# First attention of a two-block model: the reciprocal one unit late, transposes and values one unit later, and each head's values on its own half of the array's columns by turns

## The reference, cut to what matters

```
rows = s // GRID_W                      # 16 rows of 64 tokens
row_start = np.clip(r - kh // 2, 0, rows - kh)
scores = jnp.einsum('bhrnqd,bhrnikd->bhrnqik', q_blk, kg).astype(jnp.float32)
scores = scores + bias[None]
scores = jnp.where(valid[:, :, None, :], scores, -1e30)
probs = jax.nn.softmax(scores, axis=(-2, -1)).astype(v.dtype)
out = jnp.einsum('bhrnqik,bhrnikd->bhrnqd', probs, vg)
```

## Time and profile before

| what | value |
|---|---|
| median of three executions | 4185.94 us |
| the profiled execution's own time | 4187.09 us |
| its span in the trace | 4185.3 us |
| TensorE busy over the span | 3963.6 us, 95% |
| VectorE, ScalarE, GpSimd busy | 43%, 25%, 17% |
| the attention of this change | about 192 to 387 us of the span |
| mean granted TensorE clock | 0.964 of full speed |

### The profile page before, as it was taken

One profiled execution on the slowest core, in us unless ns is written; L12 is line 12 of the kernel. 1 busy time (PEld: TensorE's weight loads), 2 busy tenths in 40 slices (PEclk: granted clock), 3 DMA queues, 4 the chain that ended last, 5 costly groups with the idle time before them and its releaser, 6 DMA issues. The chain is left out here.

```text
span 4185.3 us, 42926 instructions
## 1 busy us (share of the span) xinstructions
PE 3963.6 (95%) x16912; PEld 2751.7 (66%) x16912; DVE 1783.1 (43%) x3155; ACT 1049.6 (25%) x1797; POOL 692.6 (17%) x533
## 2 busy tenths in 40 slices
PE   8988999999999999999997998988999998999998
PEld 4465444444458888877555888745678747888886
DVE  2165776533032233224447898356642123322232
ACT  1043553000022211223332332114431112122210
POOL 1053000000001100111002011004420112333333
PEclk9999999999999999998998998899899999999999
DMA  3200102334011111122101212200002201111111
GB/s 144 58 1 3 38 10 71 101 111 141 30 41 42 50 51 51 51 72 76 53 6 29 41 31 54 96 16 1 1 23 72 85 18 60 51 51 48 44 51 51
DMA packets 200181, 211.42 MB, mean 51 GB/s; under 512 B 64560, under 2 KB 152240, under 8 KB 199600
## 3 DMA queue, kind: packets, MB, share of 16 engines
q1 hardware_dynamic: 140624, 172.50, 12.5%
q10 hardware_dynamic: 59360, 36.19, 3.2%
HBM read 185.33 MB, written 21.50 MB: 49 GB/s over the span
## 5 line engine op out<-in xcount | busy, mean ns | idle before, releaser
L95 PE MATMUL ps<-halves 128*128 128x512 f32 x7296 | 1665.0, 391 | 23.3 <-DVE halves L378 11.0
L95 PEld LDWEIGHTS ps<-halves 128*128 128x128 f32 x7296 | 1374.7, 189 | 312.2 <-issue 11.4
L95 PE MATMUL ps<-arena 128*128 128x512 f32 (+4 forms) x4208 | 1448.2, 501 | 65.2 <-DVE arena L544 25.0
L95 PEld LDWEIGHTS ps<-arena 128*128 128x128 f32 (+1 forms) x4208 | 721.9, 190 | 736.2 <-issue 667.4
L1265 DVE TENSOR_TENSOR halves<-tmps,halves 128x512 fp32r<-128x512 f32 x128 | 88.6, 692 | 525.2 <-ACT halves L1220 525.2
L1244 POOL TENSOR_TENSOR tmps<-tmps 128x512 f32<-128x512 f32 x128 | 137.7, 1076 | 1000.7 <-ACT tmps L1212 1000.7
L1151 ACT ACTIVATE halves<-raws 128x2048 fp32r<-128x2048 f32 x62 | 118.4, 1909 | 559.9 <-PE ps L95 524.6
L889 POOL TENSOR_TENSOR arena<-arena 128x512 f32<-128x512 f32 x32 | 41.9, 1311 | 939.7 <-DVE arena L860 691.2
L1251 POOL TENSOR_TENSOR arena<-arena 128x512 f32<-128x512 f32 x128 | 164.7, 1294 | 191.3 <-DVE arena L1288 191.3
L1158 DVE TENSOR_TENSOR halves<-raws,halves 128x2048 fp32r<-128x2048 f32 x62 | 142.2, 2293 | 73.6 <-ACT halves L1151 73.6
L1212 ACT ACTIVATE tmps<-ps 128x512 f32<-128x512 f32 x128 | 76.5, 598 | 377.6 <-PE ps L95 377.6
(11 more groups left out here) (272 smaller groups left out, 3549.8 us busy)
## 6 DMA issues: line engine op xcount, KB each, us to landing
arena<-in_w_in SPq DMA_DIRECT2D x16, 2048.0 KB, 9.0
raws<-in_w_ff SPq DMA_DIRECT2D x31, 1024.0 KB, 5.4
raws<-in_w_mlp SPq DMA_DIRECT2D x31, 1024.0 KB, 5.2
arena<-in_w_ada ACTq DMA_DIRECT2D x24, 1024.0 KB, 5.2
arena<-in_w_out SPq DMA_DIRECT2D x4, 2048.0 KB, 11.0
mixw<-in_w_in SPq DMA_DIRECT2D x16, 512.0 KB, 4.1
h_stash<-arena SPq DMA_DIRECT2D x1, 5120.0 KB, 20.8
inverses<-arena ACTq DMA_DIRECT2D x20, 256.0 KB, 2.9
```

Of the source, the lines that this page charges most:

```text
L95: ins = e.matmul(out_ap, l, r, start=i == 0, stop=i == n - 1)
```

## The change

Three things change, all in the four functions of the attention. First, VectorE computes the reciprocal of unit `i-1` in iteration `i`, behind bias and maximum of unit `i`. Second, transposes and evacuation are those of unit `i-3`, values and copies out those of unit `i-4`; `pbuf` gets a fifth buffer for that. Third, the values of a unit are no longer four matmuls with 128 by 128 weights but eight with 128 by 64: each head has its own 64 feature columns, 64 query rows moving, and its own half of the output partitions, the two heads by turns. Both results then lie in columns 0 to 63 of the bank, so that one copy of 128 by 64 takes the place of two of 64 by 64.

```diff
@@ tensor_natt
-            for i in range(64 + 3):
+            for i in range(64 + 4):
...
-                if 0 <= i - 2 < 64:
-                    u = i - 2
+                if 0 <= i - 3 < 64:
+                    u = i - 3
                     key = ("at", u)
...
-                if 0 <= i - 3 < 64:
-                    u = i - 3
+                if 0 <= i - 4 < 64:
+                    u = i - 4
                     r, j, start = natt_place(u)
                     key = ("ap", u)
...
-                    chain(e, o[:, 0:128], [(vals[:, start // 2 + c, j * 128:(j + 1) * 128], ptb[u % 3][:, c, :])
-                                           for c in range(4)]).then_inc(*bk.filling(key))
+
+                    for c in range(4):
+                        for s in range(2):
+                            f = slice(64 * s, 64 * s + 64)
+                            ins = e.matmul(o[f, 0:64], vals[:, start // 2 + c, j * 128 + 64 * s:j * 128 + 64 * s + 64],
+                                           ptb[u % 3][:, c, f], start=c == 0, stop=c == 3)
+                    ins.then_inc(*bk.filling(key))
@@ vector_natt
-                    e.wait_ge(*a_ex.at(i + 1))
+                u = i - 1
+                if 0 <= u < 64:
+                    c = statn[:, u % 8, :]
+                    e.wait_ge(*a_ex.at(u + 1))
                     e.reciprocal(c[:, 2:3], c[:, 1:2]).then_inc(*a_rc.tick())
-                if 0 <= i - 3 < 64:
-                    u = i - 3
+                if 0 <= i - 4 < 64:
+                    u = i - 4
...
-                    e.tensor_copy(QB[0:64, j, r, 0, :], bk.tile(key)[0:64, 0:64])
-                    e.tensor_copy(QB[64:128, j, r, 0, :], bk.tile(key)[64:128, 64:128]).then_inc(*bk.emptying(key))
+                    e.tensor_copy(QB[:, j, r, 0, :], bk.tile(key)[:, 0:64]).then_inc(*bk.emptying(key))
@@ scalar_natt
-                    if i >= 4:
-                        e.wait_ge(*bk.full(("at", i - 4)))
-                    e.activation(pbuf[i % 4], sb[i % 2], ACT.Exp, bias=c[:, 0:1],
+                    if i >= 5:
+                        e.wait_ge(*bk.full(("at", i - 5)))
+                    e.activation(pbuf[i % 5], sb[i % 2], ACT.Exp, bias=c[:, 0:1],
...
-                if 0 <= i - 2 < 64:
-                    u = i - 2
+                if 0 <= i - 3 < 64:
+                    u = i - 3
```

More of the change, by code:

```diff
@@ L474, in build @@
         sb = [R(T0 + i * 512, 512) for i in range(2)]
-        pbuf = [R(T0 + 1024 + i * 512, 512) for i in range(4)]
-        ptb = [R3(T0 + 3072 + i * 512, 4, 128) for i in range(3)]
+        pbuf = [R(T0 + 1024 + i * 512, 512) for i in range(5)]
+        ptb = [R3(T0 + 3584 + i * 512, 4, 128) for i in range(3)]
         statn = sm[:, 8:32].rearrange("p (a b) -> p a b", b=3)
@@ L503, in tensor_natt @@
                     for c in range(4):
-                        ins = e.transpose(o[:, c * 128:(c + 1) * 128], pbuf[u % 4][:, c * 128:(c + 1) * 128],
+                        ins = e.transpose(o[:, c * 128:(c + 1) * 128], pbuf[u % 5][:, c * 128:(c + 1) * 128],
                                           ident[:, :])
                     ins.then_inc(*bk.filling(key))
-                if 0 <= i - 3 < 64:
-                    u = i - 3
+                if 0 <= i - 4 < 64:
+                    u = i - 4
                     r, j, start = natt_place(u)
@@ L542, in vector_natt @@
                     e.wait_ge(*bk.full(key))
-                    e.tensor_copy(QB[0:64, j, r, 0, :], bk.tile(key)[0:64, 0:64])
-                    e.tensor_copy(QB[64:128, j, r, 0, :], bk.tile(key)[64:128, 64:128]).then_inc(*bk.emptying(key))
+                    e.tensor_copy(QB[:, j, r, 0, :], bk.tile(key)[:, 0:64]).then_inc(*bk.emptying(key))
         def scalar_natt(e):
-            for i in range(64 + 2):
+            for i in range(64 + 3):
                 if i < 64:
@@ L567, in gpsimd_natt @@
                 e.wait_ge(*a_rc.at(i + 1))
-                e.tensor_scalar(pbuf[i % 4], pbuf[i % 4], c[:, 2:3], None, ALU.mult).then_inc(*a_sl.tick())
+                e.tensor_scalar(pbuf[i % 5], pbuf[i % 5], c[:, 2:3], None, ALU.mult).then_inc(*a_sl.tick())
         YA = QB[:, :, :, 0, :]
```

## The result

| kernel | median (us) | against before, with its 95% interval | scores apart (us) | first gate matmul of the next stage (us) |
|---|---|---|---|---|
| before | 4188.59 | 1 | 2.84 | 414.4 |
| the full change | 4150.53 | 0.9905 (0.9883 to 0.9928) | 2.33 | 383.0 |
| the same again, on another chip | 4152.10 | 0.9916 (0.9900 to 0.9931) | 2.33 | 383.1 |

The change makes the kernel about 38 us faster (medians of four runs each: 4188.59 less 4150.53; a fourth execution of the kernel before, 4195.95 us, came to the three named at the start). Forecast was 19.2. "First gate matmul" is the first record of the gates of the recurrent branch (L605 before, L612 after). It has no wait of its own in either kernel and shows what the attention alone gave: 31.4 us. In the profiled runs the spans differ by 40.8 us. The other 9.4 come behind the attention, in code that is the same in both.

The account below looks back on a forecast made before the run. VectorE with the exponential in its middle was taken as the bound, 2.84 us a unit; afterwards TensorE alone at 2.52. 60 x 0.32 = 19.2 us off 4187.09 gives 4167.9, by the median 4166.7 us; forecast's own range 4161 to 4178, range given up to 4190.

Parts of the forecast that it names:

- the term of the values: Values on TensorE: 16 passes of 64 moving columns at 0.055 us each, 0.88 us a unit, as much as before.
- side by side: Rival for the values: both array halves run at once, 16 passes take 0.44 us, gain 33.6 us, 4152 us; 15%.
- weight loads 0.03 apart: Sign in the profile after that the two heads' value passes run side by side; 0.055 would confirm the forecast.
- Loop P: TensorE alone: scores, transposes, values and two changeovers, 0.86 + 0.44 + 0.17 + 0.88 + 0.17 = 2.52 us a unit.
- The changeovers: TensorE gaps between full-width and half-width groups, ahead of and behind the values: 0.17 us each way, twice a unit.
- Loop L: Through all engines, scores to values to scores two units on: 5.00 us for two units, 2.50 a unit.
- VectorE's loop: VectorE with the exponential in its middle: the whole 2.84 us period before; 1.78 us left after the change.
- GpSimd's scaling: GpSimd needs 1.56 us a unit; its later start would be too late for the transposes only for T below 1.74.
- The count of 60 units: Intervals of the attention that get shorter: 58 between units 3 and 61, two for the end; 60 x 0.32 = 19.2 us.
- that rival: TensorE's clock falls to 0.50 for part of the attention; half of the time there gives 22 us slower, 4208 us; 4%.
- the pass at 0.107: Rival: a small value pass on TensorE costs 0.107 us, values 1.71, 30.6 us slower, 4216.5 us; 13%.
- the turns that cost: Rival: alternating tiles in the values costs time, 0.075 us a pass, 2.84 us a unit, no change, 4186 us; 12%.

Follow-up runs that it names:

- Head by head: The full change with the four value matmuls of the first head before the four of the second, not by turns; 4161.25 us, ratio 0.9933.
- evacuation first: The full change with ScalarE evacuating transposes i-3 ahead of exponential i; 4146.21 us (0.9892), again 4142.97 us (0.9897).
- the late reciprocal alone: The kernel before with only the reciprocal moved behind the next maximum; 4186.59 against 4190.29 us, ratio 0.9995.
- the pairs: From evacuation first, values and copies of two units together in every second iteration; 4127.31 us, ratio 0.9866.

## Why the prediction was wrong

The direction was right, and so was what bound the kernel before, but the size was half of what came.

**The failed step** is the term of the values: "In both rows the time follows the columns that move ... so I take the first: 0.88 for the values". Measured: 16 passes at 0.0275, 0.44. The step lined the passes of both halves up one behind the other; they run side by side, eight on each half at 0.058. That columns set the pace of a pass held on each half (0.058 for 64 moving, 0.109 for 128). The row it was taken from, has its passes on one tile until one change halfway, so its average says little of passes by turns. Yet it was misread: the prediction says that the change halfway shows nothing and that the two tiles "do not overlap to be seen", but the single loads of that very group show the second tile starting beside the last three passes of the first. Head by head, the case nearest to this row, gave 0.87 for values and changeover, where 1.05 was forecast for the two. The rival *side by side*, at 15% the less likely, had the mechanism: 2.28 a unit and 33.6 us against 2.33 and 31.4 at the gates, 32.8 from the first values. Its sign, weight loads 0.03 apart, is the one that came. Its argument against, that 0.055 may be what two instructions cost to issue, is refuted by the full change itself, where two cost 0.0275.

**Loop P** came out at 2.11 in place of 2.52 and is no longer the bound. The changeovers were right in sum, 0.34 forecast and 0.37 measured (0.10 at the scores, 0.10 at the transposes, 0.17 behind the values), but they lie in three places, not two. That the sum is so near is in part luck: 0.17 was forecast ahead of the values, where 0.10 came, and 0.17 behind them, where 0.27 came.

**Loop L** was right: forecast 5.00 for two units with values of 0.88, that is 4.56 with 0.44; measured 4.67. Most of the missing 0.11 is the slower scores, 1.16 to the bias in place of 1.07. It is this loop that the full change runs into, and evacuation first showed it by cutting it.

**VectorE's loop** was right for the kernel before; the copy was mis-sized, 0.35 for what was taken out of it in place of 0.21, which costs nothing in the full change, where VectorE waits. That GpSimd's scaling is early enough was right too: its count (late only for T below 1.74) says when a wait begins, and at 2.33 there is none. The expectation of the late reciprocal alone took the same count for the period, and there it failed.

**The count of 60 units** held nearly: 60 x 0.511 = 30.7 against 31.4 at the gates and 32.8 from the first values, 60 x 0.908 = 54.5 against 53.9 and 57.3 for the pairs. The close fit at the gates has some luck in it, from the early landing in the kernel before. The clock stayed at 1.00, so that rival did not come; nor did the pass at 0.107 or the turns that cost.

**What stays open**: what makes up the 0.17 behind the last half-width pass; why one copy holds VectorE for so much less than two; and what sets the granted clock of an execution, which moves the program by more than some of the differences looked for here.

## What to carry to other kernels

With several engines in a ring, write down every loop with the number of units that it spans; a wait that is removed uncovers the next loop, and here the cheapest gain (an exchange on ScalarE) lay in a loop that the change had not touched. Small matmuls on different column halves should stand by turns, not one head after the other. And stretches of half-width passes should be few and long: each one cost 0.37 us in all, which ate most of the 0.45 (0.89 less 0.44) that a single unit's halves had saved. Before two kernels are told apart by a few us, their granted clocks should be compared, and an average over a group of passes should be taken apart into single starts before a cost is read from it.

## What the runs showed of the hardware that was not expected

- Passes of 128 rows by 64 columns on one column half start 0.058 us apart with 64 columns moving and 0.109 with 128, whether the other half works or not; on alternating halves that makes 0.0275 and 0.048 on average. The Trainium skill ("TensorEngine Tiling (Array Packing)", Tiling Modes, Key Properties) says that different tiles can load weights and multiply in parallel, and that a change of mode drains the engine. These runs agree with the first (loads on the two halves 0.012 us apart). The 0.37 us of each half-width stretch fits the second, though no run shows the drain itself.
- Weight loads of the second head start up to three passes before the first head's are through, though they stand behind them in the program (head by head, 0.287 against 0.402).
- Behind full-width work the first weight load of the scores starts 0.11 us ahead of its matmul; behind half-width passes the two start together.
- Executions of one kernel differ by some 3.4 us for each 0.001 of mean granted clock (4195.52 us at 0.963, 4174.74 at 0.969).
- A copy of 128 by 64 out of PSUM let the next operation of VectorE start 0.12 us after its own start, while the second of two copies of 64 by 64 held it for 0.26. The reason was not looked for.
- The same transfer of the shifted copy landed at 208.4 to about 212 us from run to run, with the same instructions ahead of it, and moves the whole attention with it.
